# One-core encoder step with a PEER expert lookup: GpSimd asks u rows 22 (at the end 7) slots ahead of v rows, the last two heads are weighted in parts of four, and the closing products are gone

## The chip, the cores and the metric

One Trainium2 chip, one of its cores. The metric is the device time of one execution in microseconds (us), as the median of several runs. Less is better.

## The reference, cut to what matters

The kernel computes one layer of a streaming encoder for 384 tokens: 256 of a prompt and 8 x 16 of samples. They make three blocks t = 0, 1, 2 of 128 tokens. A block goes through a projection, a gated recurrence (group A), a sparse attention (group B), the output projection, and last a retrieval of experts ("PEER"), which is what the change touches:

```python
def peer(xn, wq, subkeys, u, v):          # n = tokens, 8 heads, 16 experts each
    q = xn @ wq                           # per head, in two halves
    s = q . subkeys; sv, si = top_k(s, 16)
    cand = sv[0] + sv[1]; fv, fi = top_k(cand, 16)
    eidx = ...                            # 16 rows of a table of 16384 rows
    g = softmax(fv)
    ue, ve = u[eidx], v[eidx]             # rows of 1024 float32
    act = gelu(sum_d x[n, d] * ue[n, h, k, d])
    return sum over h, k of (g * act)[n, h, k] * ve[n, h, k]
y = h + peer(rmsnorm(h))
```

Each token takes 8 heads x 16 = 128 experts, so each needs 128 rows of u and 128 rows of v of 4096 bytes.

## The kernel before, in words

**Slots.** The PEER part runs in 384 slots, numbered 0 to 383: 3 blocks x 8 heads x 16 experts. One slot handles, for the 128 tokens of a block at once, one row of u and one row of v per token: a gather of 128 x 4096 bytes for u (line 506) and one for v (line 514). "u row n" and "v row n" below mean such a gather for slot n. For each slot the engines do this:

- GpSimd (POOL) asks for both rows. Its loop (lines 521 to 529) walks over v rows; before v row n it asks u rows until n + 1 + LAG - max(0, (n - 312) // 6) of them are asked, LAG = 28. A u row waits until the dot product eight u rows earlier is done (`u_free`, RU = 8 buffers), a v row until the products six slots earlier are done (`v_free`, RV = 6 buffers). The queue is in order: a waiting request holds back all that follow.
- VectorE (DVE) computes the dot products of u row n with the block's x (line 1244), which it reads from PSUM.
- ScalarE (ACT) applies gelu to the 16 dot products of a head (line 835); it does this for head i + 1 after the 12th slot of head i. DVE multiplies by the gates (line 1236); it does this for head i - 1 after the third dot product of head i. So the weights of slots 16i to 16i + 15 exist once dot product 16i + 18 is done.
- ACT makes a diagonal matrix from a column of weights (line 843, ND = 6 buffers, so it runs up to six slots ahead of TensorE), and TensorE (PE) multiplies it with the v row and sums in PSUM banks 6 and 7 (line 1643: two calls a slot, each two instructions in the trace, so four a slot).

**The other work, woven in.** All the rest of the blocks 1 and 2 (projection, recurrence, attention, choice of experts) is written out by hand as generators that yield slot numbers: an engine's piece with due slot k is issued when that engine reaches slot k. The three engines count differently: PE issues pieces up to slot n + 28 (`trunks(n + LAG)`, line 1646) after the products of slot n; ACT issues pieces up to n + 22 (`fronts(n + LAG - ND)`, line 847) after the diagonal of slot n; DVE issues the pieces of slot n after the dot product n (line 1246). The pieces wait for each other by semaphores. Those that the prediction speaks of:

- PE slot 51 `keys_and_dots(1)` (lines 1358 to 1364) waits for `key_done`, which DVE gives at the end of `keys(1)`, slot 49 (line 940). At DVE slots 42 to 49 lie also the index scores, the selection of keys (lines 955, 956) and a choice of experts.
- PE slot 64 `turned(1, ...)` waits for `normalise(1)` of DVE slot 62 (lines 978, 979).
- PE slots 91 to 94 `mixed(1, c)` (line 1420) wait for `mix_a(1)` of DVE slot 88 (lines 1014 to 1019).
- In block 2: PE 124 waits for DVE 121 (`rope`), PE 152 for DVE 149 (`keys`), PE 158 for DVE 155 (`penalty`), PE 174 for DVE 171 (the softmax sums), PE 215 for DVE 213 (`norm_h`).
- The choice of experts of head h of block t has DVE slots 128t + 16h - 20 to 128t + 16h - 17 (for the last head 348 to 351); ACT takes its exponentials at 128t + 16h - 17 (line 667; for the last head slot 351), once DVE has done slot 128t + 16h - 18 (`top_ready`, line 1046; for the last head 350).

**The end.** After the last slot of a block two products of zeros (line 1648) close the sums in banks 6 and 7 and tell ACT (`y_full`), which copies both banks to X (`read_y`, line 854). SyncE stores them (line 406), and PE starts the next block's sums after both copies (line 1634).

## Time and profile before

| what | value |
|---|---|
| time, median of 3 runs (lowest to highest) | 1263.51 us (1260.94 to 1264.93) |
| time of the profiled execution | 1264.69 us |
| its span in the profile | 1262.9 us |
| PE / DVE / POOL / ACT busy | 87% / 64% / 58% / 27% of the span |
| gathers of u and v | 768, 402.70 MB, 81.1% of what 16 DMA engines could be busy |
| all DMA | 470.68 MB, mean 373 GB/s |
| mean granted clock of TensorE | 0.97 |

Times are counted from the start of the span. "Idle before" in a row is the time the engine waited, and what ended it. Busy shares are averages over stages with different limits, so the views by stretch say more than the page's first line. A DMA share a little over 1 is how this view shows engines that are never idle.

### The profile page before, as it was taken

To read this page: it belongs to the slowest core of one execution; us is meant where nothing else is said; L and a number is where in the kernel's file an instruction comes from. 1 tells how busy PE (TensorE), PEld (TensorE's weight loads), DVE (VectorE), ACT (ScalarE), POOL (GpSimd) and SP (SyncE) were. 2 spreads that over 40 slices of the span, in tenths; PEclk is the share of its full clock that TensorE was granted. 3 is DMA by queue.
4 is the path that set the end of the run, shared out by engine and by line. 5 is a ranking of instruction groups with operands and counts; after the bars stand their busy time and mean duration, and the time that the engine had idled before them with its cause. 6 is when DMAs were issued, how large, how long until landed. Compare 5 with 4: busy or idle time off the path is not lost. (4 is left out here: it accounts for less than half of the span.)

```text
span 1262.9 us, 12585 instructions
## 1 busy us (share of the span) xinstructions
PE 1099.1 (87%) x3549; PEld 551.5 (44%) x3549; DVE 807.8 (64%) x2015; ACT 344.7 (27%) x782; POOL 732.6 (58%) x774
## 2 busy tenths in 40 slices
PE   6978999999999799887889999999677777788888
PEld 2765756556554354333435534534222222222233
DVE  1452799595876674949984666578667656764430
ACT  3521212532412223323331322322122222221111
POOL 0000356655666665767675766677576767777753
PEclk9988899999999899999998999999899999999999
DMA  8743499999999999999999999999999999999996
GB/s 350 315 172 152 164 416 412 412 336 328 383 374 359 404 409 402 410 398 383 410 406 388 409 409 409 408 409 408 413 409 410 410 409 410 408 409 404 409 344 233
DMA packets 126356, 470.68 MB, mean 373 GB/s; under 512 B 14664, under 2 KB 17744, under 8 KB 124112
## 3 DMA queue, kind: packets, MB, share of 16 engines
q0 software_dynamic: 110592, 402.70, 81.1%
q1 hardware_dynamic: 15696, 67.19, 13.5%
q8 instruction: 29, 0.48, 0.2%
q14 instruction: 39, 0.32, 0.1%
HBM read 465.34 MB, written 4.42 MB: 372 GB/s over the span
## 5 line engine op out<-in xcount | busy, mean ns | idle before, releaser
L1643 PE MATMUL PSUM<-UV,DIAG 128*128 128x512 f32 x1536 | 741.5, 617 | 116.8 <-DMA UV<-in_p_v,EIDX 113.9
L1244 DVE CUSTOM_DVE_ANT_0 UV<-UV,PSUM 128x1024 f32<-128x1024 f32 x384 | 462.8, 1218 | 216.5 <-DMA UV<-in_p_u,EIDX 211.7
L506 POOL DMA_INDIRECT UV<-in_p_u,EIDX x384 | 369.4, 962 | 292.4 <-DVE EIDX L1057 141.5
L1643 PEld LDWEIGHTS PSUM<-UV,DIAG 128*128 128x128 f32 x1536 | 275.0, 192 | 521.0 <-DMA UV<-in_p_v,EIDX 275.6
L514 POOL DMA_INDIRECT UV<-in_p_v,EIDX x384 | 362.3, 944 | 224.8 <-PE PSUM L1643 98.7
L843 ACT ACTIVATE DIAG<-CST,WGT 128x128 f32<-128x128 f32 x384 | 152.1, 400 | 723.2 <-PE PSUM L1643 719.9
L1283 PE MATMUL PSUM<-WR,XW 128*128 128x512 f32 (+1 forms) x128 | 50.6, 555 | 0.0
L1292 PE MATMUL PSUM<-XW,WR 128*128 128x256 f32 x192 | 42.3, 379 | 0.0
L1292 PEld LDWEIGHTS PSUM<-XW,WR 128*128 128x128 f32 x192 | 36.5, 190 | 6.7 <-issue 1.8
L1283 PEld LDWEIGHTS PSUM<-WR,XW 128*128 128x128 f32 x128 | 24.2, 190 | 25.2 <-issue 22.5
L1244 DVE DVE_READ_ACCUMULATOR2_ANT DOTS<- 128x1 f32 x384 | 31.6, 82 | 0.0
L1005 DVE SCALAR_TENSOR_TENSOR WR<-WR,SMALL,PSUM 128x128 f32<-128x128 f32 x84 | 23.5, 343 | 8.4 <-PE PSUM L1373 8.0
L835 ACT ACT_TABLE_LOAD x22 | 28.2, 1283 | 0.4
L179 DVE MAX8 SEL<-UV 128x8 f32<-128x128 f32 (+1 forms) x72 | 21.9, 332 | 9.7 <-ACT UV L537 7.0
L1283 PE MATMUL PSUM<-UV,XNT 128*128 128x512 f32 (+1 forms) x64 | 28.0, 600 | 0.0
L1014 DVE RECIPROCAL WR<-WR 128x512 f32<-128x512 f32 x3 | 10.1, 3353 | 27.4 <-ACT WR L537 27.4
L667 ACT ACT_TABLE_LOAD x20 | 25.7, 1283 | 1.6 <-DVE SEL L1046 1.2
L1373 PE MATMUL PSUM<-AIV,WR 32*128 32x128 f32 x192 | 21.7, 308 | 4.5 <-ACT WR L612 4.5
L1373 PEld LDWEIGHTS PSUM<-AIV,WR 32*128 32x128 f32 x192 | 18.2, 209 | 16.4 <-issue 16.3
L1292 PE MATMUL PSUM<-XNT,UV 128*128 128x128 f32 x192 | 25.0, 298 | 0.0
L1292 PEld LDWEIGHTS PSUM<-XNT,UV 128*128 128x128 f32 x192 | 24.7, 213 | 0.5 <-issue 0.2
L1393 PEld LDWEIGHTS PSUM<-SQ,WR 128*128 128x128 f32 x176 | 23.3, 212 | 2.4 <-issue 2.4
(220 smaller groups left out, 856.8 us busy)
## 6 DMA issues: line engine op xcount, KB each, us to landing
UV<-in_p_u,EIDX POOLq DMA_INDIRECT x384, 10.8
UV<-in_p_v,EIDX POOLq DMA_INDIRECT x384, 10.8
WR<-in_p_wq SPq DMA_DIRECT2D x10, 512.0 KB, 7.0
UV<-in_w_B SPq DMA_DIRECT2D x2, 2048.0 KB, 12.5
UV<-in_w_o SPq DMA_DIRECT2D x2, 2048.0 KB, 8.0
UV<-in_p_wq SPq DMA_DIRECT2D x2, 2048.0 KB, 7.8
WR<-in_w_B SPq DMA_DIRECT2D x2, 2048.0 KB, 10.0
XW<-in_w_o SPq DMA_DIRECT2D x8, 512.0 KB, 6.8
```

Source lines behind the costliest of these rows:

```text
L506: nc.gpsimd.indirect_dma_start(UBUF[n % RU], None, a["p_u"], bass.IndirectOffsetOnAxis(EIDX[:, n:n + 1], 0)).then_inc(u_got[n % RU], 16)
L514: nc.gpsimd.indirect_dma_start(VBUF[n % RV], None, a["p_v"], bass.IndirectOffsetOnAxis(EIDX[:, n:n + 1], 0)).then_inc(v_got[n % RV], 16)
L667: own.done(nc.scalar.activation(ex, ex, ACT.Exp, accum_out=GSUM[:, h % 2:h % 2 + 1]), gate_exp)
L835: nc.scalar.activation(GELU[:, :], DOTS[:, i % 2, :], ACT.Gelu).then_inc(gelu_done, 1)
L843: nc.scalar.activation(DIAG[:, n % ND, :], IDENT, ACT.Copy, scale=WGT[:, i % 2, s:s + 1]).then_inc(diag_ready, 1)
L1005: ins = v.scalar_tensor_tensor(out=new[:, h, :], in0=old[:, h, :], scalar=EBE[:, t, h, b:b + 1], in1=pb[:, h * P:(h + 1) * P], op0=ALU.mul ...
L1244: v.tensor_tensor_reduce(out=row, in0=row, in1=XNP, scale=1.0, scalar=0.0, op0=ALU.mult, op1=ALU.add, accum_out=DOTS[:, i % 2, s:s + 1]).t ...
L1283: ins = mm(pb[:, 0:n], x[:, c, :], w[:, c, :], start=c == 0, stop=c == KC - 1)
L1292: ins = mm(pb[:, k * n:(k + 1) * n], w[:, c, h * P:(h + 1) * P], src, start=c == 0, stop=c == KC - 1)
L1373: ins = mm(pb[:, cols], KE[t][rows, b % 2, cols], AIV[t][rows, cols], start=True, stop=True)
L1393: ins = mm(pb[:, h * P + b * BLK:h * P + (b + 1) * BLK], S[:, h, :], SQ[t][:, h, b * BLK:(b + 1) * BLK], start=False, stop=(b, h) == (7, A ...
L1643: ins = mm(bank[6 + k][:, :], DIAG[:, n % ND, :], VBUF[n % RV][:, k * 512:(k + 1) * 512], start=False, stop=False)
```

## The change

POOL's loop no longer uses LAG: the lead of u over v is 22 up to slot 300, falls by one every five slots and is 7 from slot 371. LAG = 28 stays for PE, and ACT keeps n + 22. The last two heads (slots 352 to 383) get gelu and weights in parts of four slots: ACT takes the gelu of a part just before the first diagonal of it, DVE multiplies after the second dot product of the next part. The two products of zeros at each block's end are dropped: the last real product closes each sum. ACT waits for bank 7 by `v_free`, and at the very end DVE copies bank 7 while ACT copies bank 6.

```diff
--- before.py
+++ after.py
@@ -35,6 +35,10 @@
 SLOTS = PH * PK
 RU, RV, ND = 8, 6, 6
 LAG = 28
+
+AHEAD, AHEAD_END = 22, 7
+
+FINE, PART = 22, 4
 QR = 4
 
 MASKED, PICKED, DUMMY, DROP = -3.0e38, -3.3e38, 3.0e38, -1.0e30
@@ -323,7 +327,7 @@
         v_got = [sem(f"v_got{s}") for s in range(RV)]
         u_free, v_free, go, gelu_done, wgt_done, diag_ready = [
             sem(n) for n in ("u_free", "v_free", "go", "gelu_done", "wgt_done", "diag_ready")]
-        y_full, y_ready, y_out = sem("y_full"), sem("y_ready"), sem("y_out")
+        y_full, y_ready, y_last, y_out = sem("y_full"), sem("y_ready"), sem("y_last"), sem("y_out")
 
         def take(eng, name):
             b, turn = PLACE[name]
@@ -402,7 +406,10 @@
             def store_y(t):
                 for n in range(2):
                     cols = slice(n * 512, (n + 1) * 512)
-                    sp.wait_ge(y_ready, 2 * t + n + 1)
+                    if (t, n) == (2, 1):
+                        sp.wait_ge(y_last, 1)
+                    else:
+                        sp.wait_ge(y_ready, 2 * t + n + 1)
                     sp.dma_start(a["y"][t * P:(t + 1) * P, cols], X[t][:, cols]).then_inc(y_out, 16)
 
             sp.dma_start(X[0], a["x"][0:P]).then_inc(x_in[0], 16)
@@ -519,7 +526,7 @@
             take(pool, ("wo", 0, 1))
             asked = 0
             for n in range(HEADS * PK):
-                while asked < min(HEADS * PK, n + 1 + LAG - max(0, (n - 312) // 6)):
+                while asked < min(HEADS * PK, n + 1 + max(AHEAD_END, AHEAD - max(0, (n - 296) // 5))):
                     if asked == 4:
                         take(pool, ("qq", 0, 3))
                     gather_u(asked)
@@ -830,14 +837,19 @@
                 trunks(slot)
                 gated(slot)
 
-            def gelu(i):
-                act.wait_ge(u_free, (i + 1) * PK)
-                nc.scalar.activation(GELU[:, :], DOTS[:, i % 2, :], ACT.Gelu).then_inc(gelu_done, 1)
+            def gelu(i, lo=0, hi=PK):
+                act.wait_ge(u_free, i * PK + hi)
+                nc.scalar.activation(GELU[:, lo:hi], DOTS[:, i % 2, lo:hi], ACT.Gelu).then_inc(gelu_done, 1)
 
             def weigh(i):
-                act.wait_ge(wgt_done, i + 1)
+                if i < FINE:
+                    act.wait_ge(wgt_done, i + 1)
                 for s in range(PK):
                     n = i * PK + s
+                    if i >= FINE and s % PART == 0:
+                        if n > FINE * PK:
+                            gelu(i, s, s + PART)
+                        act.wait_ge(wgt_done, FINE + (n - FINE * PK) // PART + 1)
                     if n >= ND:
                         act.wait_ge(v_free, n - ND + 1)
                     nc.scalar.activation(DIAG[:, n % ND, :], IDENT, ACT.Copy, scale=WGT[:, i % 2, s:s + 1]).then_inc(diag_ready, 1)
@@ -845,12 +857,18 @@
                         read_y(i // PH - 1)
                     if n >= ND:
                         fronts(n + LAG - ND)
-                    if s == 11 and i < HEADS - 1:
-                        gelu(i + 1)
+                    if s == 11 and i < FINE:
+                        if i < FINE - 1:
+                            gelu(i + 1)
+                        else:
+                            gelu(FINE, 0, PART)
 
             def read_y(t):
-                for n in range(2):
-                    act.wait_ge(y_full, 2 * t + n + 1)
+                for n in range(2 if t < 2 else 1):
+                    if n == 0:
+                        act.wait_ge(y_full, t + 1)
+                    else:
+                        act.wait_ge(v_free, SLOTS * (t + 1))
                     own.done(nc.scalar.activation(X[t][:, n * 512:(n + 1) * 512], bank[6 + n][:, :], ACT.Copy), y_ready)
 
             for slot in range(LAG):
@@ -1231,9 +1249,14 @@
                 gated(slot)
                 chosen(slot)
 
-            def weights_of(i):
-                dve.wait_ge(gelu_done, i + 1)
-                v.tensor_tensor(WGT[:, i % 2, :], GELU[:, :], GATE[:, i * PK:(i + 1) * PK], ALU.mult).then_inc(wgt_done, 1)
+            def weights_of(k):
+
+                dve.wait_ge(gelu_done, k + 1)
+                i, lo, hi = k, 0, PK
+                if k >= FINE:
+                    i, lo = FINE + (k - FINE) * PART // PK, (k - FINE) * PART % PK
+                    hi = lo + PART
+                v.tensor_tensor(WGT[:, i % 2, lo:hi], GELU[:, lo:hi], GATE[:, i * PK + lo:i * PK + hi], ALU.mult).then_inc(wgt_done, 1)
 
             for n in range(HEADS * PK):
                 i, s = n // PK, n % PK
@@ -1244,9 +1267,13 @@
                 v.tensor_tensor_reduce(out=row, in0=row, in1=XNP, scale=1.0, scalar=0.0,
                                        op0=ALU.mult, op1=ALU.add, accum_out=DOTS[:, i % 2, s:s + 1]).then_inc(u_free, 1)
                 fronts(n)
-                if i and s == 2:
+                if i and s == 2 and i <= FINE:
                     weights_of(i - 1)
-            weights_of(HEADS - 1)
+                if i >= FINE and s % PART == 1 and n > FINE * PK + PART:
+                    weights_of(FINE + (n - FINE * PK) // PART - 1)
+            weights_of(FINE + (HEADS - FINE) * PK // PART - 1)
+            dve.wait_ge(v_free, SLOTS * NT)
+            own.done(v.tensor_copy(X[2][:, 512:D], bank[7][:, :]), y_last)
 
         @block.tensor
         def _(pe):
@@ -1641,11 +1668,11 @@
                         pe.wait_ge(diag_ready, n + 1)
                         for k in range(2):
                             ins = mm(bank[6 + k][:, :], DIAG[:, n % ND, :], VBUF[n % RV][:, k * 512:(k + 1) * 512],
-                                     start=False, stop=False)
+                                     start=False, stop=n % SLOTS == SLOTS - 1)
+                            if k == 0 and n % SLOTS == SLOTS - 1:
+                                ins.then_inc(y_full, 1)
                         ins.then_inc(v_free, 1)
                         trunks(n + LAG)
-                for n in range(2):
-                    mm(bank[6 + n][:, :], ZERO, wide(ZERO, 1, 4), start=False, stop=True).then_inc(y_full, 1)
 
 
 def constants():
```

## Rows read from the trace of the kernel before

**Rows 1.** The page: span, busy time, the gathers' queue

```profile
span 1262.9 us, 12585 instructions
PE 1099.1 (87%) x3549; PEld 551.5 (44%) x3549; DVE 807.8 (64%) x2015; ACT 344.7 (27%) x782; POOL 732.6 (58%) x774
...
q0 software_dynamic: 110592, 402.70, 81.1%
```

**Rows 2.** Four stretches: length, engines' busy time (instructions), granted clock, DMA share, GB/s

```profile
202.00:257.00 55.00, 55.00 (x162) 28.83 (x161) 40.23 (x103) 19.85 (x40) 32.16 (x34) 1.00 1.02 413
257.00:312.00 55.00, 53.12 (x183) 32.56 (x182) 42.65 (x109) 18.30 (x40) 33.57 (x35) 1.00 0.89 321
900.00:1215.00 315.00, 248.81 (x505) 87.06 (x506) 192.35 (x459) 68.99 (x156) 223.83 (x238) 0.99 1.03 409
1215.00:1255.00 40.00, 38.77 (x90) 16.66 (x89) 3.86 (x7) 7.70 (x21) 17.79 (x19) 1.00 0.83 287
```

**Rows 3.** Timeline of POOL (start, length): u requests 23 and 51, first v request

```profile
170.71 0.94 POOL L506 DMA_INDIRECT UV<-in_p_u,EIDX  x1 [0.30 <-issue]
...
189.99 0.94 POOL L514 DMA_INDIRECT UV<-in_p_v,EIDX  x1 [0.30 <-issue]
...
257.21 0.94 POOL L506 DMA_INDIRECT UV<-in_p_u,EIDX  x1 [0.30 <-PE PSUM L1643]
```

**Rows 4.** Line 506 up to three moments: count, durations, first and last start

```profile
L506 POOL DMA_INDIRECT UV<-in_p_u,EIDX x56: 933/937/1673, 142.9 to 274.5; - x56
...
L506 POOL DMA_INDIRECT UV<-in_p_u,EIDX x69: 933/937/2872, 142.9 to 318.0; - x69
...
L506 POOL DMA_INDIRECT UV<-in_p_u,EIDX x95: 933/937/2872, 142.9 to 400.0; - x95
```

**Rows 5.** Line 506, 270 to 300 us: request to landing

```profile
DMA to landing us min/median/max: 5.1/6.1/6.5
```

**Rows 6.** DVE: timeline at slots 44 and 49; dot products up to 272.3 us

```profile
251.13 1.22 DVE L1244 CUSTOM_DVE_ANT_0 UV<-UV,PSUM 128x1024 f32<-128x1024 f32 x1
...
L1244 DVE CUSTOM_DVE_ANT_0 UV<-UV,PSUM x50: 1199/1218/1222, 150.7 to 272.2; 128x1024 f32<-128x1024 f32 x50
...
272.22 1.22 DVE L1244 CUSTOM_DVE_ANT_0 UV<-UV,PSUM 128x1024 f32<-128x1024 f32 x1
...
276.94 0.69 DVE L940 TENSOR_TENSOR SQ<-SQ,WR 128x512 f32<-128x512 f32 x1
```

**Rows 7.** PE: timeline at its slot 51

```profile
277.68 0.66 PE L1299 MATMUL PSUM<-CST,WR 128*128 128x128 f32 x4 [1.88 <-DVE SQ L940]
```

**Rows 8.** Timelines: DVE slot 62, PE 64, DVE 88, PE 91

```profile
317.74 2.29 DVE L979 TENSOR_TENSOR WR<-WR,SMALL 128x2048 f32<-128x2048 f32 x1
...
320.90 1.91 PE L1299 MATMUL PSUM<-CST,WR 128*128 128x128 f32 x16
...
396.93 3.35 DVE L1014 RECIPROCAL WR<-WR 128x512 f32<-128x512 f32 x1 [7.60 <-ACT WR L537]
...
404.68 1.88 PE L1420 MATMUL PSUM<-WR,MIXA 128*128 128x512 f32 x4
```

**Rows 9.** Line 514, 900 to 1200 us; ACT's exponentials, last head

```profile
DMA to landing us min/median/max: 9.6/11.3/14.2
...
1132.09 0.21 ACT L667 ACTIVATE SEL<-SEL 128x16 f32<-128x16 f32 x1
```

**Rows 10.** The end: v requests, last u request, PE's last run, ACT's copies

```profile
L514 POOL DMA_INDIRECT UV<-in_p_v,EIDX x364: 932/937/1417, 190.0 to 1211.6; - x182
...
1210.32 0.94 POOL L506 DMA_INDIRECT UV<-in_p_u,EIDX  x1 [0.30 <-issue]
...
1222.54 36.32 PE L1643 MATMUL PSUM<-UV,DIAG 128*128 128x512 f32 x84 [0.53 <-DMA UV<-in_p_v,EIDX]
...
1259.11 1.23 ACT L854 ACTIVATE X<-PSUM 128x512 f32<-128x512 f32 x2 [10.11 <-PE PSUM L1648]
```

**Rows 11.** Waits, the whole span: in total, times, longest us

```profile
POOL UV L514 <- DVE DOTS L1244: 48.2, 74, 3.7
```

## The prediction

> **What bounds the kernel now.** I read first the page [rows 1]: no engine is busy over 87%, but the gathers alone move 402.70 MB in 768 requests, so 0.524 MB each. The view by stretch tells why that matters [rows 2]: from 900 to 1215 us the DMA engines are never idle at 409 GB/s. There a u or v row costs 0.524 / 409 = 1.28 us, a slot 2.56. Two stretches are not of that kind. From 202 to 257 PE is busy 55.00 of 55 us and from 257 to 312 it is 53.12, while the DMA share falls to 0.89: PE works off block 1's pieces and sets the pace. At the end, 1215 to 1255, only v rows are left and the share is 0.83: PE needs 36.32 us for 84 instructions, 1.73 us a slot, against 1.28 for a v row [rows 10].
>
> The run of 36.32 us is also what the chain of waits ends with. So a change can win at the end, where the DMA engines idle, and lose where PE's own stretch gets longer. The views of the two requests' order and of who waited show where.
>
> **Term 1: the lead of u, 28 down to 22.** v row n waits for the products of slot n - 6 and u row n + 28 stands before it in POOL's queue. With 22, u row j is asked at the moment at which u row j + 6 is asked now. PE still issues its pieces 28 slots ahead, and these wait for DVE's pieces of nearly the same slots, which DVE can only reach after the dot product of that slot. Three such places lie in PE's stretch:
> - *PE slot 51 on DVE slot 49.* The dot product of slot 49, the 50th, starts at 272.22 and its keys end 5.41 us later, at 277.63; PE has waited 1.88 us for just that [rows 6, 7]. Its margin is gone already. With the change u row 49 is asked when the 56th is now, at 274.5 [rows 4], and lands 6.1 us later [rows 5], at 280.6: the keys end at 286.0 at the earliest, +8.4. But DVE is behind too: row 44 would be asked at 257.21 [rows 3], land at 262.3 at the least (5.1, rows 5) and not be worked on from 251.13 [rows 6]; the 26.5 us of work from there to the keys' end, nearly without a pause, end at 288.8 (+11.2), and the landings of 45 and 46 (6.1 again) add some 2. Between +8.4 and +13.5 I take +13, as the backlog is what the rows show.
> - *PE slot 64 on DVE slot 62.* The 69th request is at 318.0 [rows 4]; plus 6.1, 1.2 for the dot product and 2.5 for the softmax sums (2.29 and a short reciprocal, rows 8) gives 327.8, where PE starts at 320.90: +7. With the shortest landing +6.
> - *PE slot 91 on DVE slot 88.* The 95th request is at 400.0; plus 6.1, 1.2 and 4.9 (reciprocal 3.35, two operations behind it) gives 412.2, where PE starts at 404.68: +7.5. Here PE's stretch ends, and the requests in flight (about ten, 12.8 us, less some 5 to start anew) land meanwhile; I keep 1 and bound it by 0 and 7.5.
>
> Sum +21 (low 10, should the later two hide behind the first; high 28).
>
> The first v row could go out at 171.9 instead of 189.99 [rows 3], but the first product starts at 202.7 behind PE's own pieces, and PE is full from there: nothing. The six u rows fewer in stock when PE's stretch ends are 6 x 1.28 = 7.7 us of transfer to be made up later: +7.7, or nothing if PE's stretch does not bind.
>
> **Term 2: block 2's pieces.** PE 124, 158, 174 and 215 wait for DVE two or three slots before. There the DMA queue is 11.3 us deep [rows 9], so a stall idles the DMA engines only for what exceeds the queue: a u row needs at least 5.1 + 1.2 and the piece itself, 2 to 5 us, against 2 or 3 slots of 2.56 us. That is 1 to 3 us at each, and PE 152 has DVE late already. I take +4, between 0 and 14.
>
> **Term 3: the lead's way down, slots 296 to 352.** The parts of four begin at slot 352 only. The diagonal of slot 336 still needs dot product 354, 18 ahead, but the lead there is 14; u row 354 is asked before v row 340, so after the products of slot 333. And ACT, after the diagonal of 329, waits for the last choice of experts, DVE slot 350, whose u row is asked before v row 335, after the products of slot 328. Now both are long past: these exponentials run at 1132.09 [rows 9]. From the request it is 1.2 (v row before it) + 11.3 + 1.2 + 1.7 (table load and exponentials) = 15.4 us to the diagonal 330, and PE has one slot, 2.6: it stands for 13, of which a queue 11.3 deep with a floor of 5.1 hides 6. Left: 7. At 336 the same sum leaves 4. Term +11; bounds 2 and 22.
>
> **Term 4: the end.** Now the last u row is asked at 1210.32, before v row 363 [rows 10], and PE has 84 / 4 = 21 slots left. With a lead of 7 it stands before v row 376, so 8 are left: 13 slots go from PE's pace to the DMA's, 13 x (1.73 - 1.28) = -5.8. That holds if the parts are in time: a part needs the dot product five slots after its first, the lead plus POOL's five v rows is twelve, and 7 x 1.73 = 12 us cover the 5.1 + 1.2 + 1. While ACT waits at a part's start its diagonals stand behind it, and PE lives on the six made before; DVE's product with the gates holds the dot products behind it, but only for a gelu already asked. Six more gelus and six more such products (about 0.2 us each, estimated from the smallest operations shown) lie in idle time: PE, not they, sets the pace. If they are late, this term is 0.
>
> **Term 5: zeros and copies.** PE's last product ends at 1222.54 + 36.32 = 1258.86 and ACT's first copy starts at 1259.11 [rows 10]: 0.25 us for the zeros, and one of the two copies (1.23 for both) goes beside the other, 0.6: together -0.9. At the two block changes it lies under the DMA queue.
>
> **Sum.** 21 + 7.7 + 4 + 11 - 5.8 - 0.9 = +37.0. The profiled execution took 1264.69 around a span of 1262.9; 1264.69 + 37.0 = 1301.7, and 1.2 less against the median of the runs, 1263.51: 1300.
>
> Term 1 rests on the landing time. The Trainium skill (DMA: Bandwidth & Descriptors, Anatomy of one DMA) gives a gather by GpSimd as about 2.0 us + bytes / 436e3, an estimate of 3.2 us here. By that each wait of terms 1 and 3 would be 2 us shorter and the sum some 8 less; the rows, with 5.1 as the least, decide.
>
> **Rivals.**
> - *The early waits hide.* DVE works ahead less but also idles less, and only the lead's descent costs. For: DVE itself waits 7.60 us for ACT before slot 88's piece [rows 8], and a later start eats into that. Against: PE already waits 1.88 us at slot 51. 7.7 + 11 - 5.8 - 0.9 = +12.0: 1275. Chance 0.14.
> - *Faster.* A v request stands behind a u request that waits for a dot product: 48.2 us in 74 waits [rows 11]. A shorter lead frees it, and if DVE still ends the keys of slot 49 before PE's slot 51, the lead costs nothing. Then -5.8 - 0.9, and of the 0.14 x 55 = 7.5 us that the DMA engines idle from 257 to 312 some regained: 1250 to 1257. It decides at 277.7 us. Against: from 900 to 1215 us no DMA engine is idle, so the waits there cost nothing, and PE's wait at slot 51 is already for DVE. Chance 0.12.
> - *Gains and waits cancel*, within 0.3% (4 us, what a measurement of this kernel can tell from no change): 0.04.
> - *The lead does nothing*, since the 8 u buffers stop POOL first: only the end's -6.7. Against: at 274.5 u row 55 goes out [rows 4], though dot product 49, started at 272.22 [rows 6], would soon let row 57 go; it is the lead that holds them. Its 0.02 are in faster.
> - *Worse*: stalls feed each other, above 1324: 0.04.
>
> **Numbers.** Forecast 1300, own range 1281 to 1324, chance 0.66. With the first rival's 0.14 that makes 0.80 from 1268 to 1324; faster, same and worse are left out. Faster 0.12, same 0.04, slower 0.84.
>
> **What would show it.** Right: PE waits ten or more us for line 940's counterpart near 276 us; DVE's waits for u rows grow in 200 to 420; near slots 330 and 336 ACT waits for DVE and the DMA share dips; PE's last run without a pause is near 32 instructions. Wrong: PE's piece of slot 51 starts by 280, or the DMA share stays at 1.03 around slot 330.

## The result, and the profile after

The changed kernel takes 1394.78 us (median of 4 runs, 1390.56 to 1397.43) against 1264.22 us before (4 runs, 1260.94 to 1266.24): ratio 1.1027, 95% interval 1.1002 to 1.1051. It is slower by 130.6 us; the forecast was slower by 37, with the range up to 1324. The direction was right, the size wrong by more than three times.

The page of the changed kernel (time of this execution 1395.34), to be read beside [rows 1]:

```profile
span 1393.5 us, 12591 instructions
PE 1124.4 (81%) x3543; PEld 574.6 (41%) x3543; DVE 809.2 (58%) x2022; ACT 336.6 (24%) x787; POOL 729.6 (52%) x774
...
q0 software_dynamic: 110592, 402.70, 75.0%
```

The work is the same to the byte. What grew is idle time: the gathers' packets took 0.811 x 1262.9 = 1024 us before and 0.750 x 1393.5 = 1045 us now, so about 110 of the 131 us are time in which the DMA engines moved no packet of the gathers. Of the busy times PE's grew most, by 25.3 us, with six instructions fewer; the last section comes back to that.

The view by stretch answers to [rows 2] (columns as there). The first two stretches are the same as there, then come two more in which the share is low:

```profile
202.00:257.00 55.00, 50.73 (x136) 24.71 (x135) 31.82 (x85) 24.57 (x47) 27.12 (x29) 0.94 0.83 320
257.00:312.00 55.00, 40.33 (x141) 26.82 (x140) 39.35 (x105) 9.65 (x19) 21.97 (x24) 0.88 0.71 261
450.00:500.00 50.00, 34.10 (x72) 15.47 (x73) 30.65 (x72) 9.51 (x21) 20.18 (x22) 0.75 0.90 342
1225.00:1285.00 60.00, 28.52 (x49) 11.12 (x50) 24.53 (x65) 6.08 (x16) 25.14 (x27) 0.73 0.70 261
```

From 257 to 312 us PE was busy for 53.12 us with 183 instructions before, now 40.33 with 141, and the DMA share fell from 0.89 to 0.71. No engine is the bound in that stretch any more: PE and DVE are each busy 40 of 55 us, and PE, DMA and DVE wait for one another.

**Where the time came from.** A first, small part lies at the first product of the PEER part (the kernel before, then the changed one):

```profile
202.71 7.03 PE L1643 MATMUL PSUM<-UV,DIAG 128*128 128x512 f32 x16
```

```profile
206.19 10.05 PE L1670 MATMUL PSUM<-UV,DIAG 128*128 128x512 f32 x16 [3.63 <-ACT DIAG L855]
```

It starts 3.5 us later, for ACT's diagonals, and the same 16 instructions take 3.0 us more; the granted clock from 202 to 210 us is 0.71, for 1.00 before. The forecast had nothing here.

Then PE's timeline, all its waits of 4 us or more for a DVE piece or an ACT piece between 276 and 1200 us (in brackets the wait before the instruction):

```profile
297.86 1.11 PE L1326 MATMUL PSUM<-CST,WR 128*128 128x128 f32 x4 [14.67 <-DVE SQ L958]
353.60 3.68 PE L1326 MATMUL PSUM<-CST,WR 128*128 128x128 f32 x16 [6.15 <-DVE WR L997]
393.19 2.04 PE L1400 MATMUL PSUM<-AIV,WR 32*128 32x128 f32 x8 [4.00 <-DVE WR L1023]
452.61 3.78 PE L1447 MATMUL PSUM<-WR,MIXA 128*128 128x512 f32 x4 [8.51 <-DVE MIXA L1037]
492.81 1.97 PE L1326 MATMUL PSUM<-CST,XW 128*128 128x128 f32 x8 [13.29 <-DVE XW L1048]
571.49 2.40 PE L1326 MATMUL PSUM<-CST,ZB 128*128 128x128 f32 x10 [9.84 <-DVE ZB L924]
652.84 1.11 PE L1326 MATMUL PSUM<-CST,WR 128*128 128x128 f32 x4 [8.92 <-DVE SQ L958]
689.55 0.41 PE L1568 MATMUL PSUM<-PEN,CST 128*128 128x272 bf16 x1 [8.70 <-ACT WR L780]
725.57 1.54 PE L1326 MATMUL PSUM<-CST,WR 128*128 128x128 f32 x6 [8.26 <-DVE WR L1183]
862.65 1.97 PE L1326 MATMUL PSUM<-CST,XW 128*128 128x128 f32 x8 [9.64 <-DVE XW L1048]
959.24 1.67 PE L1400 MATMUL PSUM<-AIV,WR 32*128 32x128 f32 x8 [4.24 <-DVE WR L1023]
```

Eleven waits, 96.2 us. The first is the counterpart of [rows 7], which waited 1.88 us. The delay against the kernel before grows with them. Against [rows 7] and [rows 8] PE's piece of slot 51 starts at 297.86 for 277.68 (+20.2), that of slot 64 at 353.60 for 320.90 (+32.7), that of slot 91 at 452.61 for 404.68 (+47.9). ACT's last exponentials were ready to run at 1253.78 - 27.47 = 1226.3, for 1132.09 in [rows 9] (+94.2): all of that before slot 330, where the forecast had +32.7 (terms 1 and 2: 21 + 7.7 + 4).

Why hardly a transfer runs meanwhile is in POOL's timeline at the first of these waits:

```profile
287.84 0.94 POOL L521 DMA_INDIRECT UV<-in_p_v,EIDX  x1 [0.30 <-issue]
289.09 0.94 POOL L513 DMA_INDIRECT UV<-in_p_u,EIDX  x1 [0.30 <-issue]
303.37 0.94 POOL L521 DMA_INDIRECT UV<-in_p_v,EIDX  x1 [13.34 <-PE PSUM L1670]
```

The next v row needs a buffer that only PE's products free; PE stands at the piece; and every u row behind that v row in the queue stands too. So DVE gets no further rows to work ahead with while PE waits for DVE. The next margin is not refilled.

**Slots 314 to 352.** ACT's timeline, then PE's (both of the changed kernel):

```profile
1203.49 0.22 ACT L674 ACTIVATE SEL<-SEL 128x16 f32<-128x16 f32 x1 [18.01 <-DVE SEL L1064]
...
1224.60 0.40 ACT L855 ACTIVATE DIAG<-CST,WGT 128x128 f32<-128x128 f32 x1 [1.89 <-PE PSUM L1670]
1225.02 1.28 ACT L674 ACT_TABLE_LOAD   x1
1253.78 0.22 ACT L674 ACTIVATE SEL<-SEL 128x16 f32<-128x16 f32 x1 [27.47 <-DVE SEL L1064]
...
1254.12 0.69 ACT L855 ACTIVATE DIAG<-CST,WGT 128x128 f32<-128x128 f32 x2
1254.83 1.28 ACT L842 ACT_TABLE_LOAD   x1
1267.22 0.21 ACT L842 ACTIVATE GELU<-DOTS 128x16 f32<-128x16 f32 x1 [11.11 <-DVE DOTS L1267]
1267.34 1.26 ACT L855 ACTIVATE DIAG<-CST,WGT 128x128 f32<-128x128 f32 x4
1283.88 1.28 ACT L855 ACTIVATE DIAG<-CST,WGT 128x128 f32<-128x128 f32 x4 [15.27 <-DVE WGT L1259]
```

```profile
1204.38 17.89 PE L1670 MATMUL PSUM<-UV,DIAG 128*128 128x512 f32 x36 [6.56 <-ACT DIAG L855]
...
1254.66 6.33 PE L1670 MATMUL PSUM<-UV,DIAG 128*128 128x512 f32 x8 [15.52 <-ACT DIAG L855]
1267.87 9.98 PE L1670 MATMUL PSUM<-UV,DIAG 128*128 128x512 f32 x16 [6.88 <-ACT DIAG L855]
1284.42 15.41 PE L1670 MATMUL PSUM<-UV,DIAG 128*128 128x512 f32 x32 [6.57 <-ACT DIAG L855]
```

Four waits, 35.5 us: for the exponentials of the last choice but one before diagonal 314 (they need dot product 334), for those of the last choice before diagonal 330, for the gelu of head 21 after diagonal 331 (it needs dot product 351), and for its weights at 336 (dot product 354). The forecast had the second and the fourth. The first lies before slot 330, so in the 94.2 us above; the other three are 29.0 us.

**The end.** PE's last run, ACT's one copy and DVE's, against [rows 10]:

```profile
1376.32 14.00 PE L1670 MATMUL PSUM<-UV,DIAG 128*128 128x512 f32 x32 [0.58 <-DMA UV<-in_p_v,EIDX]
...
1389.50 0.60 ACT L872 ACTIVATE X<-PSUM 128x512 f32<-128x512 f32 x1 [9.04 <-PE PSUM L1670]
...
1390.36 0.69 DVE L1276 COPY X<-PSUM 128x512 f32<-128x512 f32 x1 [13.61 <-PE PSUM L1670]
```

The last run has shrunk from 84 instructions to 32, as forecast. Yet PE ends at 1390.32 for 1258.86, +131.5, so the way from slot 330 to the end added 131.5 - 94.2 = 37.3 us, 8.3 more than the three waits there. In this stretch the transfers are the bound again (columns as in [rows 2], where 1215 to 1255 us had a share of 0.83):

```profile
1300.00:1375.00 75.00, 61.14 (x127) 22.17 (x128) 31.18 (x56) 12.45 (x37) 54.84 (x59) 1.00 1.02 407
```

### The profile page after: what moved, and what is told of

It is laid out like the page before. It is cut to its first block and busy times, and to the rows that moved or that the text cites. A ratio compares the mean times of both kernels' runs of the same rounds, so it can differ in the third digit from the quotient of the medians.

```text
span 1393.5 us, 12591 instructions
## 1 busy us (share of the span) xinstructions
PE 1124.4 (81%) x3543; PEld 574.6 (41%) x3543; DVE 809.2 (58%) x2022; ACT 336.6 (24%) x787; POOL 729.6 (52%) x774
## 5 line engine op out<-in xcount | busy, mean ns | idle before, releaser
L1670 PE MATMUL PSUM<-UV,DIAG 128*128 128x512 f32 x1536 | 753.1, 630 | 119.1 <-DMA UV<-in_p_v,EIDX 77.4
L1267 DVE CUSTOM_DVE_ANT_0 UV<-UV,PSUM 128x1024 f32<-128x1024 f32 x384 | 465.7, 1218 | 459.4 <-DMA UV<-in_p_u,EIDX 456.5
L513 POOL DMA_INDIRECT UV<-in_p_u,EIDX x384 | 365.1, 951 | 270.0 <-DVE EIDX L1075 142.8
L1670 PEld LDWEIGHTS PSUM<-UV,DIAG 128*128 128x128 f32 x1536 | 289.6, 199 | 518.2 <-issue 322.6
L855 ACT ACTIVATE DIAG<-CST,WGT 128x128 f32<-128x128 f32 x384 | 144.0, 397 | 644.4 <-PE PSUM L1670 563.1
L1326 PE MATMUL PSUM<-CST,WR 128*128 128x128 f32 (+1 forms) x84 | 16.0, 348 | 48.0 <-DVE SQ L958 23.6
L674 ACT ACTIVATE SEL<-SEL 128x16 f32<-128x16 f32 x24 | 5.2, 216 | 160.4 <-DVE SEL L1064 160.3
L1319 PEld LDWEIGHTS PSUM<-XW,WR 128*128 128x128 f32 x192 | 37.4, 196 | 11.5 <-issue 6.2
L1326 PEld LDWEIGHTS PSUM<-CST,WR 128*128 128x128 f32 (+1 forms) x84 | 12.6, 176 | 54.8 <-DVE SQ L958 25.2
L1400 PE MATMUL PSUM<-AIV,WR 32*128 32x128 f32 x192 | 23.6, 321 | 12.8 <-DVE WR L1023 8.2
L674 ACT ACT_TABLE_LOAD x20 | 25.7, 1283 | 22.4 <-DVE SEL L1064 22.1
L842 ACT ACT_TABLE_LOAD x22 | 28.2, 1283 | 0.4
L1326 PE MATMUL PSUM<-CST,XW 128*128 128x128 f32 x24 | 5.5, 407 | 26.9 <-DVE XW L1048 26.9
L1023 DVE SCALAR_TENSOR_TENSOR WR<-WR,SMALL,PSUM 128x128 f32<-128x128 f32 x84 | 23.5, 342 | 6.3 <-PE PSUM L1400 5.9
```

The costliest lines, as they stand in the source:

```text
L513: nc.gpsimd.indirect_dma_start(UBUF[n % RU], None, a["p_u"], bass.IndirectOffsetOnAxis(EIDX[:, n:n + 1], 0)).then_inc(u_got[n % RU], 16)
L674: own.done(nc.scalar.activation(ex, ex, ACT.Exp, accum_out=GSUM[:, h % 2:h % 2 + 1]), gate_exp)
L842: nc.scalar.activation(GELU[:, lo:hi], DOTS[:, i % 2, lo:hi], ACT.Gelu).then_inc(gelu_done, 1)
L855: nc.scalar.activation(DIAG[:, n % ND, :], IDENT, ACT.Copy, scale=WGT[:, i % 2, s:s + 1]).then_inc(diag_ready, 1)
L1023: ins = v.scalar_tensor_tensor(out=new[:, h, :], in0=old[:, h, :], scalar=EBE[:, t, h, b:b + 1], in1=pb[:, h * P:(h + 1) * P], op0=ALU.mul ...
L1267: v.tensor_tensor_reduce(out=row, in0=row, in1=XNP, scale=1.0, scalar=0.0, op0=ALU.mult, op1=ALU.add, accum_out=DOTS[:, i % 2, s:s + 1]).t ...
```

## The experiments

Theory T after this reading: what counts is how far POOL's u rows run ahead compared with the 28 slots by which PE issues its pieces ahead (22 for ACT). With the lead at 22 nearly every piece of DVE comes late for PE, at any stage. Rivals: the parts of four and the descent carry the loss (P); the smaller stock of rows does, wherever the pieces stand (S); ACT's waits at its exponentials do (A).

The comparisons ran on four chips, each kernel beside the kernel before on the same chip. The kernel before took 1266.18 us in the first comparison, 1365.03 in the second, 1365.02 in the third, 1353.68 in the fourth. Ratios are comparable within one; losses below are ratio minus one, times before's median there. The changed kernel was not in the first comparison: its 130.6 us are those of the result above, where the kernel before took 1264.22.

| run | comparison | median us | ratio (95% interval) |
|---|---|---|---|
| lead 22 throughout | 1 | 1362.96 | 1.0762 (1.0740 to 1.0783) |
| zeros and copies alone | 1 | 1265.79 | 0.9991 (0.9979 to 1.0002) |
| descent, parts, zeros | 1 | 1293.17 | 1.0213 (1.0190 to 1.0237) |
| changed, pieces 24 and 18 ahead | 1 | 1300.63 | 1.0269 (1.0249 to 1.0289) |
| lead 22 in slots 0 to 77 | 2 | 1402.82 | 1.0279 (1.0227 to 1.0330) |
| lead 22 in slots 78 to 295 | 2 | 1396.34 | 1.0214 (1.0161 to 1.0268) |
| changed, exponentials later | 2 | 1429.15 | 1.0472 (1.0403 to 1.0541) |
| changed, PE's pieces 25 ahead | 2 | 1388.61 | 1.0162 (1.0110 to 1.0215) |
| lead 22 in slots 0 to 77, again | 3 | 1406.24 | 1.0276 (1.0234 to 1.0319) |
| lead 22 in slots 78 to 295, again | 3 | 1392.10 | 1.0204 (1.0178 to 1.0231) |
| the changed kernel | 3 | 1454.84 | 1.0664 (1.0629 to 1.0698) |
| late descent, parts, zeros | 3 | 1363.44 | 0.9980 (0.9959 to 1.0002) |
| lead 25 throughout | 4 | 1359.93 | 1.0028 (0.9994 to 1.0063) |
| late descent, PE's pieces 25 ahead | 4 | 1362.33 | 1.0057 (1.0023 to 1.0091) |
| descent, exponentials later | 4 | 1376.11 | 1.0174 (1.0117 to 1.0231) |

**The starting lead alone.** On the kernel before:

```diff
-while asked < min(HEADS * PK, n + 1 + LAG - max(0, (n - 312) // 6)):
+while asked < min(HEADS * PK, n + 1 + min(22, LAG - max(0, (n - 312) // 6))):
```

> The kernel before, with the lead of u rows held at 22 from the start (it joins the old descent at slot 348); no parts of four, zeros kept. Theory T, that the shorter lead alone makes DVE's pieces late against PE's and ACT's, which still run 28 and 22 slots ahead: the whole delay of the changed kernel up to slot 324 is here, +95 us, and some of the next: 1350 to 1375. Rival P, that the parts of four and the steeper descent carry half of it or more: at most 1330. The forecast's own terms 1 and 2 would give +33, 1297.

Measured +96.5 us, of the changed kernel's 130.6. Inside T's 1350 to 1375; P is out, and so are the forecast's terms 1 and 2. Its view of waits shows much the same as the changed kernel's, which has 456.5, 26.9 and 23.6 us in these three lines (columns: in total, times, longest):

```profile
DVE UV L1244 <- DMA UV<-in_p_u,EIDX: 405.6, 229, 15.3
...
PE PSUM L1299 <- DVE XW L1030: 25.9, 3, 12.3
...
PE PSUM L1299 <- DVE SQ L940: 23.7, 2, 14.8
```

**Zeros and copies alone.** On the changed kernel, the old lead, and no head in parts:

```diff
-... n + 1 + max(AHEAD_END, AHEAD - max(0, (n - 296) // 5)):
+... n + 1 + LAG - max(0, (n - 312) // 6)):
-FINE, PART = 22, 4
+FINE, PART = 24, 4
-                        else:
+                        elif FINE < HEADS:
                             gelu(FINE, 0, PART)
```

> The changed kernel with the old lead (28, the old descent) and no parts of four: only the dropped zeros and the split copy of block 2 are left of the change. Both theories: within 0.3% of before, most likely 0.9 us under it (term 5).

Measured -1.1 us, between -2.7 and +0.3: it fits term 5 (-0.9) and also nothing.

**The descent.** On the changed kernel:

```diff
-... n + 1 + max(AHEAD_END, AHEAD - max(0, (n - 296) // 5)):
+... n + 1 + (LAG if n < 296 else max(AHEAD_END, AHEAD - (n - 296) // 5)):
```

> The changed kernel with the lead 28 until slot 296 and the change's way down from there (22 at 296 to 7 at 371), parts of four and dropped zeros kept. T: the delay that the changed kernel gains after slot 324, +27 to +36 us: 1291 to 1300. Rival P, that the late stages carry most: above 1330. The forecast's terms 3 to 5 would give +4.3, 1268.

Measured +27.0, 1293.17: inside T's 1291 to 1300, while the forecast's terms 3 to 5 gave +4.3. PE's timeline has the four waits again:

```profile
1101.07 18.26 PE L1670 MATMUL PSUM<-UV,DIAG 128*128 128x512 f32 x36 [6.56 <-ACT DIAG L855]
...
1151.39 6.68 PE L1670 MATMUL PSUM<-UV,DIAG 128*128 128x512 f32 x8 [15.53 <-ACT DIAG L855]
1164.31 8.78 PE L1670 MATMUL PSUM<-UV,DIAG 128*128 128x512 f32 x16 [6.24 <-ACT DIAG L855]
1180.03 18.13 PE L1670 MATMUL PSUM<-UV,DIAG 128*128 128x512 f32 x36 [6.94 <-ACT DIAG L855]
```

35.3 us of waits, 27.0 of time. Where the difference lies is seen by the start of PE's first product of a slot, counted in the traces at four instructions a slot (us; for the changed kernels, how much later than before, in the trace of each):

| slot | before | changed | descent | pieces nearer (next experiment) |
|---|---|---|---|---|
| 64 | 406.4 | +49.8 | -3.3 | +4.5 |
| 296 | 1059.6 | +96.6 | -1.8 | +15.9 |
| 312 | 1101.5 | +91.8 | -11.5 | +11.1 |
| 336 | 1158.4 | +126.1 | +21.7 | +31.4 |
| 344 | 1177.9 | +122.8 | +18.3 | +28.2 |
| 382 | 1255.3 | +131.5 | +27.7 | +36.7 |

From 312 to 336 the descent kernel loses 33.2 us for its 35.3 us of waits: next to nothing of them is hidden, with the queue full before (a DMA share of 1.02 from 1065 to 1101 us). Ahead of that it gains 9.7 us, while POOL asks for fewer u rows, and from 344 on it loses 9.4, where those rows have to be moved. The changed kernel shows the same three parts. With the starting lead's 96.5 the 27.0 make 123.5 of 130.6, so the two stages come near to adding up.

**The pieces nearer.** On the changed kernel

```diff
-LAG = 28
+LAG = 24
```

which moves PE's pieces to 24 slots ahead and ACT's to 18; POOL's lead stays:

> The changed kernel with everything it has, but PE's pieces 24 slots ahead of its products and ACT's 18, in place of 28 and 22; POOL's lead stays 22 to 7. T, that what counts is the distance between POOL's lead and the slots that PE and ACT run ahead: PE waits for DVE with four slots more between, so two thirds or more of the +95 us before slot 324 come back: 1290 to 1335. Rival S, that the smaller stock of u rows itself costs the time, wherever the pieces stand: 1380 to 1400.

Measured +34.1, 1300.63, inside T's 1290 to 1335: of 130.6 us some 96 are back, with the same 22 rows of lead. S is out. By the table 15.9 us of it lie before slot 296 and the rest on the lead's way down. It is not the lead that costs but its distance to the pieces. The first wait of PE's timeline is gone; those of 4 us or more for DVE's or ACT's pieces (there is one of 5.64 for a diagonal, too) are four, with 23.5 us, in place of eleven with 96.2:

```profile
339.28 1.11 PE L1326 MATMUL PSUM<-CST,WR 128*128 128x128 f32 x4 [5.10 <-ACT SG L544]
...
526.92 2.40 PE L1326 MATMUL PSUM<-CST,ZB 128*128 128x128 f32 x10 [6.02 <-DVE ZB L924]
...
636.36 0.41 PE L1568 MATMUL PSUM<-PEN,CST 128*128 128x272 bf16 x1 [7.12 <-ACT WR L780]
...
674.21 1.62 PE L1326 MATMUL PSUM<-CST,WR 128*128 128x128 f32 x6 [5.24 <-ACT WR L786]
```

**Early slots or middle slots.** Two edits of the kernel before, the first for the early slots, the second for the middle ones:

```diff
-... n + 1 + LAG - max(0, (n - 312) // 6)):
+... n + 1 + (22 if n < 78 else LAG - max(0, (n - 312) // 6))):
+... n + 1 + (22 if 78 <= n < 296 else LAG - max(0, (n - 312) // 6))):
```

> The kernel before, with the lead of u rows 22 only before v rows 0 to 77, and the old lead from there. Forecast terms 1 (early pieces and six rows of stock, which are asked back after slot 78): +28.7, 1295. Theory T from the traces of the changed kernel and of the one with lead 22 throughout (delay +38 at slot 72, +49 at slot 80): +38 to +52, 1304 to 1318. Rival M, that most of the 97 us comes from the late part of the waits that the missing stock sets off, and goes once the lead is back: at most +20.

> The kernel before, with the lead 22 only before v rows 78 to 295, 28 before that and the old lead behind. Forecast term 2: +4 (0 to 14), 1270. T: each wait of PE for DVE in slots 78 to 250 is a loss of its own, whatever came before: +40 to +55, 1306 to 1321. Rival M: without the early loss the DMA queue is deep and hides them: at most +15.

> e_early once more (lead 22 only before v rows 0 to 77), beside the changed kernel itself, since the first time the kernel before took 1365 us in the same comparison and the ratio was 1.028. T: +38 to +52 us over before where before takes 1266, and something like 0.3 to 0.4 of what the changed kernel loses in the same comparison.

> f_middle once more (lead 22 only before v rows 78 to 295), beside the changed kernel. T (each wait of slots 78 to 250 is a loss of its own): +40 to +55 us over before where before takes 1266; together with e_early near the +97 of lead 22 throughout. Rival M (without the early loss they are hidden): at most +15.

> The changed kernel itself, as the measure for its neighbours of this comparison: 1.10 of before where before takes 1266. Where before takes 1365 again: 1.05 to 1.10; against it the kernels with the exponentials 6 slots later (1429) and with PE 25 slots ahead (1389) can be read: T-PE says the first is no more than 15 us faster than it or slower, the second at least 25 us faster.

Early +38.1 and +37.7; middle +29.2 and +27.8; the changed kernel +90.6 on the third chip. The early loss is at T's lower end (and 0.42 of the changed kernel's, where 0.3 to 0.4 was expected), and it stays although the lead is back from slot 78. The middle loss falls below T's +40 to +55, yet far above M's 15 and the forecast's 4: most of it comes without any early loss. The two together, 65.5 us, are far from the +97 of a chip where before takes 1266; lead 22 throughout was not run on this one. 37.7 + 27.8 leaves 25.1 of the 90.6 for the descent and the end, where the first comparison, on another chip, had 27.0. That fits three stages that add up; as a sum on one chip it is not shown.

**Which wait carries it.** On the changed kernel, first ACT's exponentials and DVE's use of them later; then, in another kernel, PE's pieces nearer:

```diff
-yield 2 if (t, h) < (0, 2) else choice_slot(t, h) + 3
+yield 2 if (t, h) < (0, 2) else choice_slot(t, h) + 9
-return 4 if (t, h) < (0, 2) else choice_slot(t, h) + 5
+return 4 if (t, h) < (0, 2) else choice_slot(t, h) + 11
```

```diff
-trunks(LAG - 1)
+trunks(25 - 1)
-                        trunks(n + LAG)
+                        trunks(n + 25)
```

> The changed kernel with ACT's exponentials of each choice of experts 6 slots later (choice + 9 for + 3), and DVE's use of them 6 slots later too. In the changed kernel ACT waits 160.3 us in 16 waits at them. Rival A, that these waits hold up the diagonals and carry the loss: 40 us or more come back, at most 1355. T-PE, that PE's own pieces waiting for DVE carry it (ACT's waits in slots 72 to 320 lie beside them) and only slots 330 to 336 hang on the exponentials: 0 to 15 us come back, 1380 to 1395.

> The changed kernel with PE's pieces 25 slots ahead of its products in place of 28; ACT's stay 22 ahead of its diagonals, POOL's lead 22 to 7. T-PE: PE's waits for DVE get three slots more of margin: about half of the 95 us before slot 324 comes back, 1330 to 1360. Rival A, that what ACT waits for carries the loss: little comes back, 1380 to 1400.

The first loses 64.4 us where the changed kernel (in the third comparison, beside a kernel before of the same time) loses 90.6: 26 back, between what A (40 or more) and T-PE (at most 15) expected, so neither had it right. The second loses 22.1: 68 back. Moving PE's pieces three slots nearer takes away three quarters; ACT's waits of 160.3 us in 16 have a smaller share. In this second kernel the longest wait left at a piece of PE's is for ACT, which itself still runs 22 ahead:

```profile
659.28 0.41 PE L1568 MATMUL PSUM<-PEN,CST 128*128 128x272 bf16 x1 [11.74 <-ACT WR L780]
```

(One of 11.0 us at line 1482, near 160 us, comes before the first product and also stands in the late descent's trace, where the lead is the old one.)

**How many slots are free.** On the kernel before:

```diff
-... n + 1 + LAG - max(0, (n - 312) // 6)):
+... n + 1 + min(25, LAG - max(0, (n - 312) // 6))):
```

> The kernel before with the lead of u rows 25 from the start (it joins the old descent at slot 330). Lead 22 cost 7.6% of before on a chip where before takes 1266 (+97 us). T, each slot less brings each dependent piece of DVE one slot, 2.56 us, nearer to PE's use of it, and the waits come once a margin is gone: between 25% and 50% of that, ratio 1.02 to 1.04. Were the loss in proportion to the slots from the first on, 1.038; were there a margin of three slots, 1.00 to 1.01.

+3.8 us, between -0.8 and +8.5. T's 1.02 to 1.04 is missed, the "margin of three slots" is right: with POOL's lead three slots short of PE's 28 there is next to no loss, and nearly all of it comes with the next three. The kernel above with PE's pieces 25 and POOL's lead 22 has the same distance and points the same way: what it loses, 22.1 us, is no more than the descent's 27. Yet the trace of lead 25 is not free of waits: PE stands 5.89, 9.38, 3.90 and 8.30 us at four of its pieces, 27.5 us, where the four longest such waits in the trace of the kernel before, on another chip, come to 10.0. The time grows by 3.8. So here most of the waiting was made up for, and at lead 22 it was not; why, no run shows.

**What the descent's waits hang on.** The descent kernel, with the exponentials 6 slots later as above:

> The kernel with lead 28 up to slot 295 and the change's descent behind it (1.021 of before, +27 us, at slots 330 to 336), with ACT's exponentials 6 slots later. T, for slot 330 the forecast's mechanism: ACT's diagonals from 330 stand behind the exponentials of the last choice, and without that 8 to 18 of the 27 us come back; what is left is the wait at 336 and behind: ratio 1.007 to 1.015. Rival, that the loss there is the late dot product 354 alone: it stays at 1.019 to 1.023.

1.0174, with an interval that takes in 1.0213: this doesn't settle how the 27 us divide. The trace says why little is to be had. ACT is past the exponentials and now stands 24.07 us at head 21's gelu, and PE waits 15.62 us two slots later (332 in place of 330). It has two more such waits, 10.22 us at 1191.00 and 7.64 at 1256.51:

```profile
1239.70 0.22 ACT L842 ACTIVATE GELU<-DOTS 128x16 f32<-128x16 f32 x1 [24.07 <-DVE DOTS L1267]
```

Both theories named one cause too few: behind the exponentials stands the gelu, behind that the weights.

**A version that keeps the end and not the loss.** On the changed kernel, so that rows 350, 351 and 354 are asked as early as before; and a second one that has PE's pieces 25 slots ahead as well:

```diff
-... n + 1 + max(AHEAD_END, AHEAD - max(0, (n - 296) // 5)):
+... n + 1 + (LAG - max(0, (n - 312) // 6) if n < 330 else max(AHEAD_END, 25 - (n - 330)))):
```

> The changed kernel with the old lead up to slot 329 (28, the old descent to 25), then one slot less a slot down to 7 at 348: parts of four and dropped zeros kept, and rows 350 and 354 asked before v row 330. T: no wait of slots 24 to 336 is longer than before, and what is left is the gain of the end, terms 4 and 5: 3 to 7 us faster than before, 1260. Rival E, that the end gains nothing because the transfers put off are made later in any case (the changed kernel lost 8.7 us there in place of gaining 5.8): within 0.3% of before or slower.

> The kernel with lead 28 and the late steep descent (parts of four, dropped zeros; it was at 0.998 of before), and PE's pieces 25 slots ahead instead of 28. T: in the kernel before PE waits for DVE's and ACT's pieces little (1.88 us at slot 51), so there are 0 to 5 us to win: ratio 0.994 to 1.000. Rival: pieces made later by PE hold up DVE and ACT, which wait for them in turn: 1.005 to 1.02.

The first is 2.7 us faster than before, between 5.6 faster and 0.3 slower: no gain that these runs could tell from none, so they do not decide between T (3 to 7 us faster) and E. PE's last run is 32 instructions in it too. The second is 7.7 us slower, between 3.1 and 12.3: T's 0.994 to 1.000 is missed, and the rival's 1.005 to 1.02 is met. Its reason, that PE's later pieces hold up who reads them, was not looked for in the trace.

## Why the prediction was wrong

- **Term 1, slot 51** (+13): the wait was right, 14.67 us where 1.88 + 13 = 14.9 was expected. But the piece starts 20.2 us later, since PE also reached it later, at 283.19 for 275.80. Of these 7.4 us 3.5 lie before the first product and 3.0 in its first 16 instructions, at the lower clock. The forecast had written "PE is full from there: nothing".
- **Term 1, slots 64 and 91** (+7 and +1): slot 64 came to 32.7 - 20.2 = 12.5 and slot 91 to 47.9 - 32.7 = 15.2. The step that failed: "the requests in flight (about ten, 12.8 us ...) land meanwhile; I keep 1". There is little in flight that helps. When PE stands, POOL stops within six v rows, and the transfers run dry: POOL's 13.34 us pause above. The four waits up to slot 91 come to 33.3 us, the delay they leave (after the first 3.5 + 3.0) to 41.4. PE is the bound in much of this stretch; that its work at a lower clock after the waits (last section) makes up the rest was not measured stretch by stretch. And one of the four, for line 1023, was not on the forecast's list.
- **The stock, 7.7 us**: it fell together with the last point, and was not measured alone. The kernel with the pieces 24 ahead has the same small stock and is 15.9 us late at slot 296, so stock and its four waits (23.5 us) come to that together.
- **Term 2** (+4, bound 14): this is the largest miss. It measured 96.6 - 49.8 = 46.8 us in the trace (slots 64 to 296 in the table), out of seven waits with 62.9 us (the first, 13.29 us for `norm_h(1)`, was on no list of the forecast's), and 28 to 29 on other chips in the kernel that has only it. Failed step: "a stall idles the DMA engines only for what exceeds the queue", 11.3 us deep. A deep queue means that a row asked is late by 11.3 us, too. PE's piece of slot s waits for DVE's slot s - 2 or s - 3, whose u row was asked, with lead 22, before v row s - 25, so after the products of slot s - 31; PE reaches the piece after those of s - 28. (This is for s - 3; for s - 2 it is one slot less.) That is 3 slots or 7.7 us for a landing (8.8 us at the median between 500 and 900 us, and 5.1 to 15.3), a dot product and the piece. So each such place waits 4 to 13 us, and the queue that was to hide the wait helps to make it. With lead 28 it is nine slots, 23 us, and with 25 six, 15.4: about a landing and a piece. That this is why 25 costs next to nothing is argued, not shown: waits remain in its trace.
- **Term 3** (+11): the place and the mechanism were right, the size was not. The forecast stand of 13 us at slot 330 was 15.52; but it took off 6 for the queue, and from slot 312 to 336 the changed kernel falls back by 34.3 us for 35.5 of waits. It left out the gelu of slot 331 (6.88) and the choice before the last, at slot 314 (6.56): row 334 is asked after the products of slot 308, which leaves PE five slots, 12.8 us, for the forecast's own 15.4. And it took 4 for slot 336 (6.57). Without the subtraction its first sum alone gives 13, more than the whole term. Against these stand 4.8 us won between slots 296 and 312.
- **Term 4** (-5.8): the last unpaused run is 32 instructions as said, but from the waits' end to the last product +8.3 came where -5.8 stood. The u rows that were put off have to be moved there: from 1300 to 1375 us the DMA share is 1.02 at 407 GB/s, so up to the last eight slots the transfers set the pace, with more left to move there than in the kernel before. Where nothing waits for it (the late descent), the end and the zeros together give 2.7 us at best estimate, and it is not shown that they give anything.
- **Term 5** (-0.9): fits (-1.1), not told from zero.
- **What the prediction looked for**: the wait at slot 51, DVE's longer waits for u rows (456.5 us for 211.7 before, over the whole span), ACT's wait and the DMA share's dip at 330, and the short last run were all there. The rival "worse: stalls feed each other", above 1324, had 0.04, and its time came. That stalls feed each other is shown only in so far as PE's waits stop POOL: across stages each loses by itself.
- **Two figures of the prediction**: "5.1 as the least" is that of u rows in one stretch; over the whole trace before, the least landing is 5.1 us for a u row and 4.1 for a v row. And in the rival "faster" 0.14 x 55 is 7.7, not 7.5. Neither changes the forecast.

Shown by runs: that the starting lead alone costs three quarters, that the pieces' distance and not the lead is what counts, that PE's pieces carry most of it, that each stage loses without the others. Argued from the traces alone: the count of slots and microseconds under term 2, and why the end gained nothing. Open: the parts of four with the old lead up to the end, which was not tried (a u row would wait for a dot product behind weights that need a v row behind that u row); how the descent's loss divides between waits one behind the other; and why the waits left at lead 25 cost so little.

## What to carry to other kernels

Where one queue feeds an engine that works ahead, and other engines issue pieces a fixed number of slots ahead, compare the two distances before changing either: request to result in microseconds (landing in the loaded queue, plus the consumer's own work) must fit into the slots between "asked" and "needed". A deep DMA queue is latency for a row that somebody waits for; count it as cover only if nothing that refills it stands behind the waiting engine. And every dependence should be listed with its margin, not only those that show up as waits today: of the eleven places where PE waited 96.2 us here, four had waited 1.88 to 3.55 us before, and at the other seven the timeline before shows no wait.

## What the runs showed of the hardware

- **TensorE's work behind the waits ran at a lower clock.** The 48 f32 products of one kind behind the waits took 418 ns at the median where they took 273 before; the lines of both kernels, the one before first:

```profile
L1299 PE MATMUL PSUM<-CST,WR x48: 272/273/329, 277.7 to 651.4; 128*128 128x128 f32 x40, 128*16 128x128 f32 x8
```

```profile
L1326 PE MATMUL PSUM<-CST,WR x48: 272/418/476, 297.9 to 736.9; 128*128 128x128 f32 x40, 128*16 128x128 f32 x8
```

  In the stretch from 450 to 500 us the granted clock is 0.75 with PE busy 34.10 of 50 us, in the same stretch before it was 1.00 with 47.10. So part of it ran at the lower of the engine's two levels, 1.2 for 2.4 GHz. PE's 25.3 us more busy time with six instructions fewer and its mean granted clock of 0.92 for 0.97 fit this. The forecast had no term for it.
- **Chips differ.** The kernel before took 1266 us on one chip and 1354 to 1365 on three others. In the stretch from 900 to 1100 us two kernels that are within 3% of before show 399 GB/s at a DMA share of 1.01 (the descent kernel, first comparison) and 373 at 0.98 (the late descent, third):

```profile
900.00:1100.00 200.00, 156.73 (x320) 56.00 (x318) 123.87 (x317) 44.03 (x96) 138.08 (x147) 0.99 1.01 399
```

```profile
900.00:1100.00 200.00, 150.63 (x329) 57.15 (x328) 127.64 (x322) 40.27 (x92) 129.34 (x137) 0.96 0.98 373
```

  The same change came to 1.10 of before in the result and 1.07 in the third comparison. What makes the chips differ was not looked into.
- **A gather's landing time has a least value near 4 us.** Between 276 and 300 us, with the transfers near to running dry, a u row took 5.1 us at least from request to landing, the number of [rows 5] again, and the v row asked at 303.37, behind POOL's pause of 13.34 us, took 4.4. Over the whole trace the least is 4.0 us for a v row and 4.5 for a u row. The Trainium skill (DMA: Bandwidth & Descriptors, Anatomy of one DMA) fits a DMA issued by GpSimd with about 2.0 us + bytes / 436e3, an estimate of 3.2 us for 0.524 MB. The trace does not agree: its least is 0.8 us above that, and from 500 to 900 us a u row's median was 8.8.
